# Two layer norms of a two-block transformer kernel: six of eight mean subtractions moved from VectorE to GpSimd

## What is computed

```python
x = _layer_norm(ALPHA * x + g1 * y, ln_g[l, 0], ln_b[l, 0])     # norms 0 and 2, for l = 0 and 1
h = x * (1.0 + sc2) + sh2
y = _conv_ffn(h, ffn_w_up[l], ffn_conv_w[l], ffn_conv_b[l], ffn_w_down[l])
x = _layer_norm(ALPHA * x + g2 * y, ln_g[l, 1], ln_b[l, 1])     # norms 1 and 3
```

## Time and profile before

| | |
|---|---|
| median of 3 runs | 2794.54 us (2805.15, 2794.54, 2791.83) |
| the profiled execution | 2792.61 us, its span 2791.3 us |
| mean granted TensorE clock | 0.969 |
| TensorE matmuls busy | 2599.2 us, 93% of the span |
| VectorE busy | 1749.7 us, 63% |
| ScalarE busy | 1072.7 us, 38% |
| GpSimd busy | 34.6 us, 1%, 38 instructions |

### The profile page before, as it was taken

The page is one execution under the profiler, slowest core; times in us unless marked ns, Lnnn a source line. Parts: engine busy times, 40 slices in busy tenths (PEclk is TensorE's granted clock), DMA queues, the critical chain, the costliest instruction groups (busy, mean ns, idle before and its releaser), DMA issues.

```text
span 2791.3 us, 32675 instructions
## 1 busy us (share of the span) xinstructions
PE 2599.2 (93%) x13380; PEld 2169.6 (78%) x13380; DVE 1749.7 (63%) x2401; ACT 1072.7 (38%) x1467; POOL 34.6 (1%) x38
## 2 busy tenths in 40 slices
PE   5987899999999999889989999999999887999998
PEld 4776778888868888678867788888887666788887
DVE  6786588888778877757624655235534675564563
ACT  3434454233454244432243533123315454442342
POOL 0010000000100000010000000000000000000000
PEclk9986999999999999999999999999999998999999
DMA  8620258755235666211111112112121100233232
GB/s 320 219 89 1 96 168 285 242 175 175 76 101 188 202 203 203 84 54 35 43 37 46 53 61 70 62 59 68 62 68 47 38 23 8 83 98 106 86 105 82
DMA packets 79700, 294.29 MB, mean 105 GB/s; under 512 B 8752, under 2 KB 10416, under 8 KB 79296
## 3 DMA queue, kind: packets, MB, share of 16 engines
q1 hardware_dynamic: 79552, 292.21, 32.5%
HBM read 290.08 MB, written 2.10 MB: 105 GB/s over the span
## 4 chain that ended last, share of the span: by engine, by line
PE 85%; DVE 8%; ACT 4%; issue 1%; DMA 1%; POOL 0%; SPq 0%; ACTq 0%; DVEq 0%
PE ps L336 70%; PE ps L361 4%; PE ps L790 3%; PE ps L2805 1%; PE ps L2773 1%; DVE w_lo L315 1%; DVE p_lo L3075 1%; PE ps L2202 1%; DVE anm L3057 1%; PE ps L1139 1%; PE ps L1699 1%; DVE h_lo L543 0%; PE ps L2786 0%; DVE x L1503 0%; ACT h_hi L537 0%
## 5 line engine op out<-in xcount | busy, mean ns | idle before, releaser
L336 PE MATMUL ps<-h_hi,w_hi 128*128 128x512 f32 (+1 forms) x2400 | 809.1, 373 | 14.4 <-DVE w_lo L315 8.4
L336 PE MATMUL ps<-h_lo,w_hi 128*128 128x512 f32 (+1 forms) x2400 | 798.4, 368 | 0.0
L336 PE MATMUL ps<-h_hi,w_lo 128*128 128x512 f32 (+1 forms) x2400 | 797.7, 368 | 0.0
L315 DVE TENSOR_TENSOR w_lo<-w_raw,w_hi 128x1024 fp32r<-128x1024 f32 (+2 forms) x319 | 414.0, 1298 | 474.6 <-ACT w_hi L307 473.7
L307 ACT ACTIVATE w_hi<-w_raw 128x1024 fp32r<-128x1024 f32 (+2 forms) x319 | 356.4, 1118 | 820.0 <-PE ps L336 781.9
L336 PEld LDWEIGHTS ps<-h_hi,w_hi 128*128 128x128 f32 x2400 | 452.8, 189 | 99.3 <-DVE w_lo L315 12.8
L336 PEld LDWEIGHTS ps<-h_lo,w_hi 128*128 128x128 f32 x2400 | 454.7, 189 | 76.9 <-issue 2.9
L336 PEld LDWEIGHTS ps<-h_hi,w_lo 128*128 128x128 f32 x2400 | 454.3, 189 | 76.4
L336 PE MATMUL ps<-g_hi,w_hi 128*128 128x512 f32 (+1 forms) x880 | 295.8, 369 | 0.8 <-DVE w_lo L315 0.8
L336 PE MATMUL ps<-g_hi,w_lo 128*128 128x512 f32 (+1 forms) x880 | 294.8, 368 | 0.0
L336 PE MATMUL ps<-g_lo,w_hi 128*128 128x512 f32 (+1 forms) x880 | 294.8, 368 | 0.0
(11 more groups left out here) (401 smaller groups left out, 2735.1 us busy)
## 6 DMA issues: line engine op xcount, KB each, us to landing
w_raw<-in_up SPq DMA_DIRECT2D x176, 512.0 KB, 3.7
m_raw<-in_w_mod SPq DMA_DIRECT2D x96, 512.0 KB, 3.7
w_raw<-in_down SPq DMA_DIRECT2D x64, 704.0 KB, 4.2
m_raw<-in_ada_w SPq DMA_DIRECT2D x83, 512.0 KB, 4.7
w_raw<-in_in SPq DMA_DIRECT2D x39, 512.0 KB, 3.7
w_raw<-in_out SPq DMA_DIRECT2D x16, 512.0 KB, 3.7
m_start<-in_ada_w SPq DMA_DIRECT2D x13, 512.0 KB, 11.6
w_raw<-in_qkv SPq DMA_DIRECT2D x12, 512.0 KB, 3.6
```

Source lines behind the costliest of these rows:

```text
L315: dve.tensor_tensor(k.w_lo[s][:, 0:w], k.w_raw[s][:, 0:w], k.w_hi[s][:, 0:w].bitcast(F32), ALU.subtract).then_inc(*k.tick("w_lo", g))
L336: last = pe.matmul(k.ps[:, product_bank(g, bank) if place is None else place, 0:tn], a[:, c, :], b[:, c, t0:t0 + tn], start=c == 0 and n = ...
```

## The change

In norms 0 and 2 GpSimd subtracts the mean from tiles 2 to 7. VectorE keeps tiles 0 and 1, and its multiply of tile f waits for GpSimd's semaphore where f is 2 or more. GpSimd's part waits for the mean and then issues its six subtractions in order. They share the semaphore that `pool_scaled` counts on. Norms 1 and 3 are as they were.

```diff
     for f in range(KD + 1):
         if f < KD:
             x = k.x[:, f, LATS]
-            dve.wait_ge(*k.seen("recentered", (which, f)))
+            dve.wait_ge(*k.seen(*recentered(which, f)))
             dve.tensor_tensor(x, x, k.rstd[:, LATS], ALU.mult).then_inc(*k.tick("scaled", (which, f)))
-        if f + 2 < KD:
+        if f + 2 < KD and recentered(which, f + 2)[0] == "recentered":
             dve_recenter(k, which, f + 2)
...
+def recentered(which, f):
+
+    return ("pool_scaled", (which, f)) if which in (0, 2) and f >= 2 else ("recentered", (which, f))
+
+
+def pool_recenter(k, which):
+    pool = k.nc.gpsimd
+    pool.wait_ge(*k.seen("mean", which))
+    for f in range(2, KD):
+        x = k.x[:, f, LATS]
+        pool.tensor_tensor(x, x, k.mean[:, :], ALU.subtract).then_inc(*k.tick(*recentered(which, f)))
...
 def pool_program(k):
     pool_start(k)
     pool_hgrn(k)
+    pool_recenter(k, 0)
     pool_scaled(k)
+    pool_recenter(k, 2)
     pool_gla(k)
```

## The result

The changed kernel takes 2804.55 us in the median of 20 runs (2798.78 to 2815.21), the one before 2793.32 in the median of 20 (2789.92 to 2805.15). The ratio is 1.0029 with a 95% interval of 1.0017 to 1.0040: slower by 8.1 us, and by 4.7 to 11.2 with the interval (the two medians are 11.2 apart). The prediction had 2798 in a range of 2788 to 2807: slower, by 5.

A forecast was written before the change was run, and what follows sets the result against it. TensorE, 93% busy, bounds the kernel, but VectorE sets the pace early in each norm. Norms +1.8 and +2.5, clock +0.7, together +5.0 on 2792.61 make 2797.6, stated as 2798; range 2788 to 2807.

The forecast's parts named there:

- The mechanism: Norms 0 and 2: GpSimd's reads hold VectorE at each change of its instruction; +3 to +8 us, chance 0.60.
- B: Rival, both norms: GpSimd and VectorE don't collide, or GpSimd enters only while VectorE waits; -2.4 to -5.6 us, chance 0.14.
- C: Rival, both norms: GpSimd let in only at every third change, as in the pool mixer; 2792 to 2796, chance 0.18.
- D of the prediction: Rival, both norms: GpSimd fetches code for its new instruction behind the mean; +7.4 us on top, 2805, chance 0.08.
- The walk: Step-by-step schedule of each norm with GpSimd's turns: first plain product 1.8 us later, then 2.5, together +4.3.
- The hold H: Time one two-input GpSimd subtraction stops VectorE in the norms: taken as 1.0 us, ends 0.41 and 1.52.
- The clock: TensorE's rise to 2.4 GHz around the norms may come later: +0.7 us for both norms together.
- What was said to cost nothing: Later tiles' waits, GpSimd's queue, DMA and SP's queue, norms 1 and 3, VectorE's late modulation jobs: no cost.

The follow-up runs named there:

- beside_tt: Kernel before, plus six two-input GpSimd subtractions of 128x512 constants per norm into a buffer nobody reads; VectorE keeps all its subtractions; ratio 1.0070.
- pool_split: psum_all with the weight split moved to GpSimd, between its tiles 3 and 4; 2788.41 us, ratio 0.9983.
- order: Kernel before, no GpSimd work in the norms; in norms 0 and 2 VectorE writes h_lo(f-1) ahead of subtracting tile f+2; ratio 1.0004.
- beside_memset: beside_tt with GpSimd's six instructions as memsets of 128x512, writes without SBUF reads; 2792.47 us in one run.
- before_psum: Control: kernel before, without GpSimd's subtractions, with reciprocal root and modulated tile in PSUM; ratio 1.0003.
- psum_all: psum, with VectorE's subtractions 0 and 1 taking the mean from PSUM and the weight split moved behind h_lo(1); ratio 0.9999.
- beside_ts: beside_tt with GpSimd's six instructions as one-input TENSOR_SCALAR 128x512 with constants as scalars; 2810.08 us in one run.
- psum: Changed kernel with reciprocal root and modulated tile in PSUM in norms 0 and 2; ratio 0.9985 to the kernel before.

## Why the prediction was right

**The mechanism was right.** The forecast was turns at each change of VectorE's instruction, and the rows show them six times in a row. They say more for it than the time does: a range of 19 us is wide for a change of 8.1, and 2804.55 lies 2.5 below its upper end. VectorE's instructions "stretched from 0.68 to about 1.7 each" are 1.75; GpSimd's subtractions "1.6 to 2.2 between VectorE's" are 1.70 to 2.24; the first h_lo "about 3.8 later" started 3.08 later and, being stretched itself, ended 4.15 later. Its evidence was in the trace before, in another phase of the program.

**The rivals.** B (no collision) is refuted by the timeline after and by beside_tt. C (every third change) came from the mixer, which I read as three reads, and the reading fits: constants in place of columns bring GpSimd in at every change. The subtraction has no columns, so C didn't apply. D of the prediction, code fetched behind the mean, is refuted: the first subtraction starts 0.76 behind the mean's start and shows only the turn.

**Two terms were too small.** The walk gave +1.8 and +2.5, with +0.7 for the clock, 5.0 in all; the profile has 3.39 and 4.45, 7.84.

- The hold H: taken as 1.0, measured 1.07. By the walk the last h_lo should have ended 21.4 behind the variance instruction, it ended at 21.87: 0.5 a norm, 1.0 in both (0.4 of it is there at the second h_lo, six turns at 0.07; the rest is ScalarE's tiles, 1.37 to 1.47 where the walk had 1.38). GpSimd's undisturbed instruction, in pool_split, takes 1.28; the hold is 1.07 of it. The figure of the Trainium skill (GPSIMD Engine Reference, section "Performance versus the Vector engine"), 4497 ns at 2048 elements, an estimate of 1.1 at 512, was nearer than my value, though it is for the whole instruction, which takes 1.28 here. The Trainium skill's rule that the pair of ports is held for the whole instruction (SBUF — State Buffer, section "SBUF: two separate sides") is one that the runs bear out in part only: VectorE was held for 1.07 of 1.28, and for 0.41 of 0.76 by the one-input instruction.
- The clock: +0.7 forecast for both norms, 2.5 found, as what is left of 7.84 without the walk's 4.3 and the 1.0. I let the last h_lo set the end, as if TensorE had caught up by then. It had not: 39 matmuls were still to come at 16.32, the first six took 2.6 us at the low clock and the other 33 took 7.5, and so the pair ended at 26.4, 5.2 behind the start of the last h_lo. At the full clock alone the walk would have been right: 15 matmuls behind an h_lo that ends at 21.87 make 25.3, 39 from 16.32 make 25.2.

**What was said to cost nothing.** Nothing speaks against it. From the plain product of norm 0 to norm 2's variance instruction it took 406.2, where it was 405.0 before, and 404.5 to 406.0 in the kernels order, beside_memset and before_psum, so that only some tenths stand outside what the clock and chance give there. The two norms cover the 8.1 of the runs within its interval.

**What the prediction said of the measurement was too cautious.** It held that a change under 0.5% can't be told from none; with 20 runs of each kernel the 0.29% stands clear of it (0.17% to 0.40%).

## What to carry to other kernels

Before work is moved to GpSimd, ask what VectorE reads meanwhile: a two-input GpSimd instruction stopped every VectorE instruction with two SBUF inputs for 1.07 us per 512 columns, against 0.60 for doing the same work on VectorE, so the move lost in a stretch that VectorE paces. With one of VectorE's operands in PSUM for that stretch the same move won, by 0.15% (0.04% to 0.26%), and by 0.17% (0.07% to 0.27%) once no two-input SBUF read of VectorE was left there. And where an engine of the kernel before has already run beside another one, its stretched records price the collision ahead of any change.

## What the hardware showed that I had not expected

GpSimd's scalar columns cost it time beside VectorE: 2.33 us with two columns and 1.15 with constants, for the same 128x512 instruction. VectorE loses the same 2.5 us to six of them either way, only later (first h_lo at 6.91 and 8.57, last at 20.05 and 20.07).

TensorE has a second pace at the full granted clock. Two stretches of 30 us in the second block's feed-forward, which no kernel here changed: the first line from the kernel before, the second from beside_tt.

```profile
2000.00:2030.00 30.00, 30.00 (x175) 26.43 (x174) 17.82 (x26) 11.19 (x13) 0.00 (x0) 1.00 0.22 73
```
```profile
2000.00:2030.00 30.00, 30.00 (x172) 26.03 (x171) 15.49 (x22) 11.27 (x15) 0.00 (x0) 1.00 0.23 70
```

172 matmuls for 175 at a granted clock of 1.00 makes about 10 us over the 540 us in which it lasted (1590 to 2130 in beside_tt). It is no matter of missing records: from one pair of matmuls of 256 columns to the next it takes 0.354 there and 0.347 in the kernel before, the mean over 10 us from 2000 on. The profiled executions of before_psum, psum_all and beside_ts have it too, before_psum among them, where GpSimd has no work in the norms; those of before, after, psum and pool_split don't. What sets it is not settled by these runs.
